# A wait on landings ahead of every fourth expert gather that GpSimd issues

## The reference

```python
sc1, i1 = lax.top_k(s1, PEER_TOPK)
sc2, i2 = lax.top_k(s2, PEER_TOPK)
cand = (sc1[..., :, None] + sc2[..., None, :]).reshape(blk, PEER_HEADS, PEER_TOPK * PEER_TOPK)
top_sc, top_c = lax.top_k(cand, PEER_TOPK)
experts = e1 * N_KEYS + e2
gate = jax.nn.softmax(top_sc, axis=-1)
u_sel = u_tab[experts]
act = jax.nn.gelu(jnp.einsum('nd,nhkd->nhk', xt, u_sel).astype(jnp.float32), approximate=False)
z = (gate * act).astype(xt.dtype)
return jnp.einsum('nhk,nhkd->nd', z, v_tab[experts])
```

## Time and profile before

| | |
|---|---|
| median of three runs | 1845.31 us |
| profiled execution, span from the first to the last instruction | 1822.2 us |
| what lies around the span (median of the runs less span; the profile has no time of its own for it) | 23.1 us |
| GpSimd busy | 1088.7 us, 60% |
| TensorE busy | 1105.9 us, 61% |
| VectorE busy | 1060.3 us, 58% |
| bytes moved | 643.9 MB, 353 GB/s over the span |

### The profile page before, as it was taken

How to read it: one execution, slowest core, us unless ns; L and a number is a source line. 1 busy time by engine, 2 the same in 40 slices (tenths; PEclk the granted TensorE clock), 3 DMA queues, 4 the chain that set the end, 5 groups by cost and what they waited for, 6 DMA issues and landing times.

```text
span 1822.2 us, 16621 instructions
## 1 busy us (share of the span) xinstructions
PE 1105.9 (61%) x5557; PEld 544.7 (30%) x5557; DVE 1060.3 (58%) x2708; ACT 273.3 (15%) x660; POOL 1088.7 (60%) x1194
## 2 busy tenths in 40 slices
PE   9766999987787789963433367543433344343345
PEld 8764444445665575540000011100000000000011
DVE  5454776737575484876677848764647444444420
ACT  3332144303210242210000000000000000000000
POOL 5523355655536555667666666666666766666664
PEclk9887998999878899996565578755565566665657
DMA  7777698999998999999999899999999999999997
GB/s 244 270 256 286 246 345 327 381 363 354 389 336 321 373 370 386 407 414 385 366 364 363 343 360 385 355 372 375 370 370 388 382 365 367 384 365 371 372 371 295
DMA packets 178652, 643.92 MB, mean 353 GB/s; under 512 B 21728, under 2 KB 21736, under 8 KB 178440
## 3 DMA queue, kind: packets, MB, share of 16 engines
q0 software_dynamic: 156672, 570.49, 80.8%
q1 hardware_dynamic: 21320, 70.28, 10.7%
q10 hardware_dynamic: 576, 2.10, 0.3%
HBM read 637.24 MB, written 5.16 MB: 353 GB/s over the span
## 4 chain that ended last, share of the span: by engine, by line
PE 31%; DVE 22%; POOL 17%; another core or an unknown queue 14%; issue 13%; ACT 2%; DMA 1%; ACTq 0%; DVEq 0%; POOLq 0%
PE pp L754 14%; POOL ring L714 8%; DVE ring L1229 6%; PE y L1046 4%; PE pp L764 4%; POOL w_ring L714 3%; PE pp L835 2%; POOL C_sample L714 2%; POOL act_T L714 2%; DVE w_ring L1229 2%; DVE act_T L1229 1%; DVE C_sample L1229 1%; POOL keys_T L714 1%; DVE lists L1558 1%
## 5 line engine op out<-in xcount | busy, mean ns | idle before, releaser
L714 POOL DMA_INDIRECT ring<-in_u_experts,expert_idx x316 | 302.0, 956 | 296.9 <-issue 79.3
L714 POOL DMA_INDIRECT ring<-in_v_experts,expert_idx_by_token x342 | 328.2, 960 | 224.3 <-issue 90.0
L1229 DVE SCALAR_TENSOR_TENSOR ring<-ring,x_normed 128x1024 f32<-128x1024 f32 x316 | 372.2, 1214 | 112.5 <-DMA ring<-in_u_experts,expert_idx 76.1
L1046 PE MATMUL a<-ring,z_columns 128*32 128x512 f32 x660 | 213.8, 957 | 184.3 <-DMA ring<-in_v_experts,expert_idx_by_token 110.7
L754 PE MATMUL pp<-act_T,w_ring 128*128 128x128 f32 (+2 forms) x1280 | 288.6, 387 | 13.2 <-ACT act_T L1889 5.7
L1046 PE MATMUL y<-ring,z_columns 128*32 128x512 f32 x792 | 226.6, 763 | 85.2 <-DMA ring<-in_v_experts,expert_idx_by_token 51.2
L754 PEld LDWEIGHTS pp<-act_T,w_ring 128*128 128x128 f32 x1280 | 198.4, 202 | 104.3 <-issue 96.7
L1046 PE MATMUL a<-w_ring,z_columns 128*32 128x512 f32 x124 | 79.3, 956 | 74.3 <-issue 35.9
L764 PE MATMUL pp<-w_ring,act_T 128*128 128x128 f32 (+1 forms) x832 | 108.2, 289 | 20.4 <-issue 9.4
L1046 PEld LDWEIGHTS a<-ring,z_columns 128*32 128x32 f32 x660 | 37.5, 146 | 275.7 <-issue 274.6
L764 PEld LDWEIGHTS pp<-w_ring,act_T 128*128 128x128 f32 (+1 forms) x832 | 100.7, 184 | 34.0 <-issue 31.4
(11 more groups left out here) (354 smaller groups left out, 1820.7 us busy)
## 6 DMA issues: line engine op xcount, KB each, us to landing
w_ring<-in_w_all SPq DMA_DIRECT2D x104, 512.0 KB
ring<-in_v_experts,expert_idx_by_token POOLq DMA_INDIRECT x342
ring<-in_u_experts,expert_idx POOLq DMA_INDIRECT x316
ring<-in_w_all SPq DMA_DIRECT2D x8, 512.0 KB, 9.1
x_res<-in_x_prompt SPq DMA_DIRECT2D x4, 512.0 KB, 7.2
C_sample<-in_state_C SPq DMA_DIRECT2D x4, 512.0 KB
out_C_s<-C_sample ACTq DMA_DIRECT2D x4, 512.0 KB
out_y_p<-x_res SPq DMA_DIRECT2D x16, 128.0 KB
```

What stands on the lines that cost most here:

```text
L714: pool.indirect_dma_start(out=slot[s], out_offset=None, in_=a["u_experts"] if kind == "u" else a["v_experts"], in_offset=bass.IndirectOffs ...
L1046: ins = pe.matmul(total[low:low + 32, half * 512:(half + 1) * 512], zcols[:, part % 2, lo:lo + 32], rhs, start=False, stop=True, skip_grou ...
L1229: dve.scalar_tensor_tensor(out=slot[s], in0=slot[s], scalar=1.0, in1=xn_now[:, :], op0=ALU.mult, op1=ALU.mult, accum_out=dots[:, part % 4, ...
```

## The change

From the position of u224 in `PLAN` on (408), each gather at a position that is divisible by 4 gets one more wait: GpSimd holds it until the gather three positions before it has landed. That one's slot and count are looked up in `PLACE`. Positions 408, 412, ... 1084 are meant, 170 in all; each is the first gather of a four, u or v.

```diff
+PACED_FROM = PLAN.index(("u", WIDER_AT))
...
+IN_FLIGHT = 3
...
-            for kind, n in PLAN:
-                s, times, before = PLACE[kind, n]
+            for i, (kind, n) in enumerate(PLAN):
+                s, _, before = PLACE[kind, n]
...
                     pool.wait_ge(u_free, before[1] + 1)
                 elif before:
                     pool.wait_ge(v_done, before[1] // 4 * 4 + 4)
+                if i >= PACED_FROM and i % 4 == 0:
+                    at, times, _ = PLACE[PLAN[i - IN_FLIGHT]]
+                    pool.wait_ge(land[at], 16 * (times + 1))
                 at = n % (8 * PART)
```

## The result

The changed kernel takes 2147.64 us (median of four runs, 2143.92 to 2153.61), the kernel before 1845.34 us (1840.83 to 1847.48): a ratio of 1.1637, 95% interval 1.1606 to 1.1668, 302 us slower. The forecast was 1947 us. The direction and the mechanism were right; the forecast slowdown of 102 us is a third of what came, and 2147.64 lies outside the range.

A forecast was written before the change was run, and what follows sets the result against it. Expert gathers were taken to set the pace: 169 periods of 6.3 us plus 3.7 give 1068 us against 966.6, +102 us on the median of 1845.3, so 1947 us; range 1830 to 2015 us.

The forecast's parts named there:

- The bound: Gathers from u224 on: expert gathers set the pace, 1.24 us each at GpSimd's pitch plus 123 us of pauses, 966.6 us.
- The hold binds, once per four, and the period is a loop: GpSimd's wait is open when reached; the next four begins once the second gather of this four has landed.
- P = 1.24 + (issue to usable): Period per held four: step to the second gather, then its issue until usable; taken as 6.3 us, break-even 5.70.
- three rows behind a pause: TensorE starting on the second gather after a GpSimd pause, 5.35, 5.46 and 5.14 us after issue; used to size the period.
- The pauses go: Paced stretch: the DMA engines have slack in each period, so about 123 us of pauses disappear.
- 97.3 us row: Largest row of GpSimd's wait list before the change, holding most of the 123 us of pauses; long ones 4.5 to 5.9.
- rival with pauses that stay: Paced stretch: pauses may hang on gather count or TensorE's groups, not rate; 2037 us, or 1992 with half; chance 0.15.
- A short queue is a slow one: DMA with few gathers under way delivers 294 to 326 GB/s instead of 420; at 320, 6.55 us per four.
- faster rival: Paced stretch: slowness behind a pause is only its after-effect; 5.5 us per four, 34 us less, 1812 us; chance 0.15.
- P = 7.6 us as the upper bound: Period per held four if landings stay as slow as in the full queue: 1.24 + 6.4 us.
- nearest rows: Trace rows behind a pause, queue as short as under the hold: 5.1 to 5.8 us from issue to TensorE's use.

The follow-up runs named there:

- always-met hold: Changed kernel with every fourth gather waiting for its twelfth predecessor instead of its third: 1624.51 us beside 1623.08 for the kernel before, ratio 1.0004.
- swap: Changed kernel with the landing's wait on the held gather itself, the readers' wait on the separate instruction: 1999.43 us beside the changed kernel's 2043.66.
- short fill: Kernel before plus a GpSimd write of 128x288 zeros every fourth gather from u224, no hold: 1828.65 us beside 1828.29, ratio 1.0026.
- fifth predecessor with the wait on the gather: Changed kernel waiting for the fifth predecessor instead of the third, the wait on the gather itself: 1829.86 us beside 1828.29 before, ratio 1.0002.
- long fill: Kernel before plus three GpSimd zero fills, 2.7 us in all, every fourth gather from u224, no hold: 2066.12 us beside 1623.17.

## Why the prediction was right in kind and wrong in size

**The bound.** That the gathers set the pace, at GpSimd's pitch of 1.24 us with pauses on top, was right. The always-met hold on a chip without pauses shows the first part bare: 855.2 us, where I had worked out 843.

**The hold binds, once per four, and the period is a loop.** Right: three steps of 1.24 us and one longer, released by a landing. Only the longer one is 3.77 us and not 2.6.

**P = 1.24 + (issue to usable).** The form held; the size of its second term is the step that failed. I took 5.06 us for it; it is 4.97 + 1.29 = 6.26. 169 x 1.20 = 203 us, which is the 201 us between 1947 and 2147.64. The difference has three parts, and the records of the DMA engines in the trace of before, which the forecast did not use, tell them apart. In my three rows behind a pause the second gather lands 4.92, 4.92 and 4.70 us after its issue, and TensorE starts 0.43, 0.54 and 0.44 us later; the means are 4.85 and 0.47, together 5.32.

- The largest part is the return. I let GpSimd come back as fast as the engine in my rows, 0.47 us after the landing. It needs 1.29 us, 0.82 more: 139 us.
- I went 0.26 us below the rows, to 5.06, on the ground that the paced queue doesn't run quite dry. The landing came no sooner for that: 44 us.
- The landing takes 4.97 us and not 4.85: 20 us. Behind the 16 pauses of before over 4 us it is 4.93 us in the mean (4.70 to 5.29), so the rows behind a pause were the right ones for the landing.

No row of before shows GpSimd released by a landing, and none was needed to see that the rows I used had another engine in them. I wrote that the wait instruction costs nothing; when met it does cost nothing, but when it ends late the gather behind it starts 0.4 us later (median) than if it had carried that wait itself.

The Trainium skill (Perfetto Trace Analysis, Per-engine timelines) bears on this: a sequencer-only instruction is fetched, waits and executes before the next one is decoded, while a gather of GpSimd waits in a hardware queue, already decoded, and passes on to the DSPs when its semaphores are met. The swap agrees: 0.71 us with the wait on the gather, 1.11 with the wait ahead of it, and separate instructions that are passed a whole four early when their own wait is met. The same page holds that GpSimd's reported spans are unreliable and that starts should be compared with starts, as is done for the period above.

The Trainium skill's price for a single DMA (DMA: Bandwidth & Descriptors, Anatomy of one DMA), 3.2 us here, which I set aside, is met by the first gather of a four: 3.2 us in the mean from the end of its issue to its landing. The awaited second one takes 4.03. For the loop it is the wrong gather.

**The pauses go.** Right: the 97.3 us row has no successor, and the stretch takes 1271.8 and 1267.4 us on the chips with pauses, 1271.9 on one without. The rival with pauses that stay is refuted for this pace; at 5.7 us per four (short fill, fifth predecessor with the wait on the gather) they stay in part. But they are there in two of the six comparisons only: on the other chips the same gain is not to be had, and the change costs 420 us instead of 302.

**A short queue is a slow one.** Right as far as it goes. In the paced stretch the DMA share falls only from 1.03 to 0.83 while the rate falls from 417 to 281 GB/s (always-met hold against after), so the engines are busy a fifth longer for each byte. The long fill has the same, a share of 0.82 at 274 GB/s, with no wait for a landing. But the 281 GB/s are a result of the period, in which the engines also idle, and 6.55 us per four, worked out from 320 GB/s, left out GpSimd's return. The faster rival fell: P was far from 5.5.

**The range.** The text worked out P = 7.6 us as the upper bound and then let the range end at P = 6.7. The measured P is 0.10 below that bound. With P = 7.6 the sum gives 2167 us; a range that kept it would have held the time, though by luck, for that bound stood for the landings of a full queue and not for GpSimd's return. Even the nearest rows were cut short: they run up to 5.8 us, which is P = 7.0 and not 6.7. What excluded the rest was that these rows lacked GpSimd's return.

## What to carry to other kernels

On an engine that issues transfers one after the other, a wait for an earlier transfer's landing costs the latency not covered by the steps between, plus that engine's own return; take the return from that engine's rows, not from a consumer's, and let the landing's wait ride on the transfer instruction. Before pacing a queue, ask whether its issuer has slack: here GpSimd had none on the chips without pauses, and each microsecond of idle time per four gathers cost 169 us there. A loss that a profile books as an unnamed pause may be the chip's, so see the kernel on a second chip before a gain is booked against it.

## What was not expected of the hardware

The kernel before takes 1845, 1828 and 1623 us on different chips, with the runs on each within 1%. The pauses of 4.5 to 6 us, in which all engines crawl, are in the profiles of the first two and absent from those of the others. Of the 222 us between the first chip and the faster ones some 95 lie ahead of the stretch, which starts that much earlier there. What makes the pauses was not found. The page of before already put 14% of the chain that ended last down to "another core or an unknown queue"; that of after has 3%. On the chips that have them they seem to hold the gathers to 5.69 to 5.70 us per four (966.6, 967.4 and 966.6 us in three kernels with different pacing), as a cap on the mean rate near 370 GB/s would; a chip without them gives 417 GB/s over the same stretch. That it is a cap was argued from doses up to 36 us, not shown beyond.

The Trainium skill (HBM Reference, Specifications (TRN2)) says that two cores share a memory domain: one streaming alone measures well above its share of some 358 GB/s, and with both streaming each gets about that share. The 417 GB/s of the chips without pauses and the 370 of the others fit a neighbour that is idle there and busy here, but no run shows the neighbour; it is a guess.

A gather's landing depends on its company, and not only on the number: in the changed kernel the first of a four lands 3.2 us after the end of its issue and the second 4.0 us, both with about 1.9 others under way when their issue starts; the third and fourth take 4.5 and 4.7 us. In the always-met hold, with 5.5 others under way, it is 6.5 us.
